# A two-layer diffusion backbone on one core: the order of the first loads and norm, and the place of the output stage against the second expert pass

## The reference, cut to what matters

```python
def _rms_norm(x, g):
    y = xf * lax.rsqrt(jnp.mean(xf * xf, axis=-1, keepdims=True) + EPS)
    return y * g
# every sub-layer: shift, scale, gate come from c and c_ctx
m = jax.nn.silu(cond) @ w + b            # (1024 x 6144) per layer, "modulation"
h = _rms_norm(x, g0) * (1 + scale) + shift
x = x + gate * _rms_norm(sublayer(h), g1)
# even layer: [short conv | latent attention], then dense SwiGLU
# odd layer: [differential attention | Fourier mixing], then top-2-of-8 experts
for e in range(N_EXPERTS):
    out = out + gates[..., e:e + 1] * _swiglu(h, w_gate[e], w_up[e], w_down[e])
```

## Time and profile before

| | us |
|---|---|
| median of 3 runs (lowest, highest) | 1734.29 (1732.22, 1735.79) |
| the profiled execution, its own time | 1732.53 |
| its span, first to last instruction | 1730.9 |
| PE busy | 1660.6, 96% of the span |
| DVE busy | 1061.8, 61% |
| ACT busy | 942.8, 54% |
| mean granted PE clock | 0.982 of full |

### The profile page before, as it was taken

One profiled execution on the slowest core, in us unless ns is written; L12 is line 12 of the kernel. 1 busy time (PEld: TensorE's weight loads), 2 busy tenths in 40 slices (PEclk: granted clock), 3 DMA queues, 4 the chain that ended last, 5 costly groups with the idle time before them and its releaser, 6 DMA issues.

```text
span 1730.9 us, 23094 instructions
## 1 busy us (share of the span) xinstructions
PE 1660.6 (96%) x8546; PEld 1323.4 (76%) x8546; DVE 1061.8 (61%) x1380; ACT 942.8 (54%) x1367; POOL 37.9 (2%) x60
## 2 busy tenths in 40 slices
PE   5898999999999999999988999999999999999997
PEld 2785458888888888678866788888888888888885
DVE  2341232253222233454474899999999989999997
ACT  3512333352222222363375677777777777777774
POOL 0000000030000000000000100000000000000010
PEclk9899899999999999999999999999999999999999
DMA  7523375169222222263204899999999999999991
GB/s 295 213 97 136 133 283 196 58 255 401 99 96 96 97 98 97 98 235 117 79 1 194 349 421 371 395 359 403 360 402 354 396 370 392 383 376 374 375 337 58
DMA packets 67708, 426.28 MB, mean 246 GB/s; under 512 B 8624, under 2 KB 12464, under 8 KB 19760
## 3 DMA queue, kind: packets, MB, share of 16 engines
q1 hardware_dynamic: 59856, 396.93, 59.8%
q0 software_dynamic: 7776, 28.32, 4.2%
HBM read 401.62 MB, written 23.59 MB: 246 GB/s over the span
## 4 chain that ended last, share of the span: by engine, by line
PE 91%; DVE 3%; ACT 3%; DMA 2%; issue 1%; SPq 0%; ACTq 0%; DVEq 0%
PE ps L1624 26%; PE ps L1626 26%; PE ps L1625 25%; PE ps L1642 3%; PE ps L1666 2%; PE ps L1781 2%; PE ps L1675 1%; DMA raw<-in_w 1%; PE ps L2063 1%; PE ps L1830 1%; DVE small L1184 1%; PE ps L1812 1%; DMA cst<-in_cst 1%; PE ps L1828 1%; DVE wl L982 1%
## 5 line engine op out<-in xcount | busy, mean ns | idle before, releaser
L1478 DVE TENSOR_TENSOR wl<-raw,wh 128x1024 fp32r<-128x1024 f32 x522 | 615.5, 1222 | 63.2 <-ACT wh L903 56.5
L903 ACT ACTIVATE wh<-raw 128x1024 fp32r<-128x1024 f32 x522 | 523.0, 1053 | 98.0 <-PE ps L1626 98.0
L1624 PE MATMUL ps<-wh,ah 128*128 128x512 f32 (+1 forms) x800 | 310.0, 387 | 1.8 <-ACT ah L886 1.2
L1624 PE MATMUL ps<-ah,wh 128*128 128x512 f32 (+1 forms) x848 | 301.1, 355 | 6.1 <-DVE al L1096 3.3
L1626 PE MATMUL ps<-wh,al 128*128 128x512 f32 (+1 forms) x800 | 302.3, 378 | 0.0
L1625 PE MATMUL ps<-wl,ah 128*128 128x512 f32 (+1 forms) x800 | 301.8, 377 | 0.0
L1626 PE MATMUL ps<-ah,wl 128*128 128x512 f32 (+1 forms) x848 | 293.6, 346 | 0.0
L1625 PE MATMUL ps<-al,wh 128*128 128x512 f32 (+1 forms) x848 | 293.6, 346 | 0.0
L982 DVE TENSOR_TENSOR wl<-raw,wh 128x1024 fp32r<-128x1024 f32 x120 | 141.5, 1222 | 126.3 <-ACT wh L480 126.3
L1624 PEld LDWEIGHTS ps<-ah,wh 128*128 128x128 f32 x848 | 161.4, 190 | 29.5 <-issue 4.1
L1625 PEld LDWEIGHTS ps<-al,wh 128*128 128x128 f32 x848 | 161.5, 190 | 20.4 <-issue 0.7
(11 more groups left out here) (251 smaller groups left out, 1584.1 us busy)
## 6 DMA issues: line engine op xcount, KB each, us to landing
raw<-in_w SPq DMA_DIRECT2D x372, 1024.0 KB, 6.4
sent<-raw POOLq DMA_DIRECT2D x16, 512.0 KB, 24.1
back<-raw POOLq DMA_DIRECT2D x16, 512.0 KB, 25.2
x<-sent POOLq DMA_DIRECT2D x7, 512.0 KB, 12.1
back<-x POOLq DMA_DIRECT2D x7, 512.0 KB
x<-in_x SPq DMA_DIRECT2D x1, 2048.0 KB, 11.4
raw<-in_ukv SPq DMA_DIRECT2D x1, 1024.0 KB, 7.4
out<-x SPq DMA_DIRECT2D x4, 256.0 KB, 2.4
```

Of the source, the lines that this page charges most:

```text
L903: act.activation(wh[:, J % SPLITS, piece_half(h)], slot(J % SLOTS)[:, piece_half(h)], ACT.Copy).then_inc(w_hi, 1)
L1478: ins = dve.tensor_tensor(wl[:, J % SPLITS, piece_half(h)], slot(J % SLOTS)[:, piece_half(h)], wh[:, J % SPLITS, piece_half(h)].bitcast(F3 ...
L1624: pe.matmul(out, lh, rh, start=start, stop=False)
```

## The change

In the start: `cst` is issued ahead of modulation piece 1; `x` goes behind modulation piece 2. PE takes the first norm's sums two at a time, ahead of modulation pieces 3, 4, 5 and 6, and a piece now goes ahead of the columns of the piece before it. ACT takes the lambda exponentials and row 2 ahead of the squares, rows 3 to 5 between the squares, and the high part of main piece 0 ahead of the root; DVE takes that piece's low part ahead of the root and the last three normalised chunks behind the scales. In the end: the output stage becomes a function `output(no)` that runs right behind `experts(0)`, ahead of the `If`; in the `If`'s body it runs again. The last down piece does column half 0 first and signals it (`y_half`), so ACT copies bank 3 earlier. The output's loops go by column half, then token half; the squares are over 512 columns, and the first half's sum enters the second half's Ln as its bias. The result goes to a slot of `raw` (`out_x`) instead of into `x`. `rows_final` is gone.

```diff
-                if p == 2:
+                if p == 1:
+                    sp.dma_start(cst[:, :, :], cst_d).then_inc(sem("cst_loaded"), 16)
+                if p == EARLY_SLOTS:
                     sp.dma_start(x[:, :, :], x_d).then_inc(x_loaded, 16)
-                    sp.dma_start(cst[:, :, :], cst_d).then_inc(sem("cst_loaded"), 16)
@@ ACT
-            act.wait_ge(x_loaded, 16)
-            squares(N_E1, lambda k: x[:, k, :])
             act.wait_ge(sem("lam_sums"), 1)
             act.activation(small[:, 2:4], ps[:, 5, 0:2], ACT.Exp).then_inc(sem("lam_exp"), 1)
+            rows(2)
+            act.wait_ge(x_loaded, 16)
+            for k in range(KD):
+                square(N_E1, k, x[:, k, :])
+                if k % 2 and k > 1:
+                    rows(2 + k // 2)
             act.wait_ge(consts_set, 1)
-            rows(2)
+            split(0)
             root(N_E1)
-            for n in range(3, MOD_FIRST - 2):
-                rows(n)
-            split(0)
...
+                    if banks == 2:
+                        act.wait_ge(w_used, PER_EXPERT * e + at.used + 2 + pieces)
+                    else:
+                        act.wait_ge(sem("y_half"), no + 1)
...
+            def output(no):
+                act.preload_act_table_set(LN_EXP)
+                for h in range(2):
+                    cols = slice(512 * h, 512 * h + 512)
+                    for t in range(2):
+                        act.wait_ge(sem("y_sum"), 4 * no + 2 * h + t + 1)
+                        act.activation(spare_row[:, t, cols], last_row[:, t, cols], ACT.Square, accum_out=half_ss[:, 2 * h + t:2 * h + t + 1]
+                                       ).then_inc(sem("y_ss"), 1)
+                        act.wait_ge(sem("y_ss"), 4 * no + 2 * h + t + 1)
+                        if h == 0:
+                            act.activation(half_eps[:, t:t + 1], half_ss[:, t:t + 1], ACT.Identity, bias=eps[:, 0:1], scale=1.0 / D
+                                           ).then_inc(sem("y_half_eps"), 1)
+                        else:
...
+                            act.activation(out_rinv[:, t:t + 1], half_ss[:, 2 + t:3 + t], ACT.Ln, bias=half_eps[:, t:t + 1], scale=1.0 / D
+                                           ).then_inc(sem("y_root"), 1)
...
+                            act.activation(out_rinv[:, t:t + 1], out_rinv[:, t:t + 1], ACT.Exp, scale=-0.5).then_inc(sem("y_root"), 1)
+                act.wait_ge(sem("y_root"), 4 * no + 4)
+                act.activation(last_row[:, 1, 0:512], last_row[:, 1, 0:512], ACT.Copy, scale=out_rinv[:, 1:2]).then_inc(sem("y_norm_act"), 1)
+
             experts(0)
+            output(0)
             with act.If(most > P):
+                act.preload_act_table(ACT.Silu)
                 experts(1)
...
+                output(1)
@@ DVE
+            split(0)
             inverse(N_E1)
             for k in range(KD):
+                if k == 5:
+                    dve.wait_ge(sem("mod_cols"), MOD_FIRST)
+                    take_modulation(0, 0, MOD_FIRST)
+                    scale_pre(0, 0, 8).then_inc(scales_ready, 1)
                 normed(N_E1, x[:, k, :], xn[:, k, :], k)
-            split(0)
-            dve.wait_ge(sem("mod_cols"), MOD_FIRST)
-            take_modulation(0, 0, MOD_FIRST)
-            scale_pre(0, 0, 8).then_inc(scales_ready, 1)
...
+            def output(no):
+                for h in range(2):
...
+                    for t in range(2):
+                        dve.wait_ge(sem("rows_summed"), 4 * no + t + 3)
+                        dve.wait_ge(sem("y_ps"), 4 * no + 2 * h + t + 1)
+                        dve.tensor_tensor(last_row[:, t, cols], last_row[:, t, cols], ps[:, OUT_BANKS[2 * t + h], :], ALU.add
+                                          ).then_inc(sem("y_sum"), 1)
+                for t, h in ((0, 0), (0, 1), (1, 1)):
+                    cols = slice(512 * h, 512 * h + 512)
+                    dve.wait_ge(sem("y_root"), 4 * no + 2 * t + 2)
+                    dve.tensor_scalar(last_row[:, t, cols], last_row[:, t, cols], out_rinv[:, t:t + 1], None, ALU.mult
+                                      ).then_inc(sem("y_norm_dve"), 1)
...
+                        dve.scalar_tensor_tensor(out=out_x[:, k, tk], in0=ps[:, TURN_BANKS[2 * t + k // 4], (k % 4) * P:(k % 4 + 1) * P],
+                                                 scalar=scl[:, 1, 3, k, 0:1], in1=x[:, k, tk], op0=ALU.mult, op1=ALU.add
+                                                 ).then_inc(sem("out_ready"), 1)
@@ PE
             mod_cols(0)
-            sum_squares(N_E1)
-            for n in range(2, MOD_FIRST):
+            def filler(n):
+                mod_piece(n)
                 mod_cols(n - 1)
-                mod_piece(n)
+            filler(2)
+            for n in range(3, MOD_FIRST):
+                if n < 7:
+                    sum_squares(N_E1, (2 * n - 6, 2 * n - 5))
+                filler(n)
...
+                    order = [(f, c) for c in range(2) for f in range(2)] if halves else [(f, c) for f in range(2) for c in range(2)]
+                    for f, c in order:
...
+                        if halves and (f, c) == (1, 0):
+                            mm.then_inc(sem("y_half"), 1)
...
+            def output(no):
...
+                for h in range(2):
+                    if h:
+                        pe.wait_ge(sem("y_rest"), no + 1)
+                    for t in range(2):
+                        pe.matmul(ps[:, OUT_BANKS[2 * t + h], :], back_sel_T[:, t * P:(t + 1) * P], y[:, 2 * h:2 * h + 2, :], start=True, stop=True
+                                  ).then_inc(sem("y_ps"), 1)
...
             experts(0)
+            output(0)
             with pe.If(most > P):
                 experts(1)
-            pe.wait_ge(sem("rows_final"), 1)
+                output(1)
```

More of the change, by code:

```diff
@@ L1528, in _ @@
             experts(0)
+            output(0)
             with dve.If(most > P):
+                dve.wait_ge(sem("y_ps"), 4)
                 dve.memset(back_sel_T, 0.0).then_inc(sem("back_sel_T"), 1)
+                dve.wait_ge(sem("y_root"), 4)
+                dve.memset(half_ss, 0.0).then_inc(sem("ss_cleared"), 1)
                 experts(1)
-                sum_rows(3)
-            dve.wait_ge(sem("back_sel_T"), 1)
-            dve.memset(small[:, 0:1], 0.0).then_inc(sem("rows_final"), 1)
@@ L1535, in _ @@
[L1535 to L1551, removed]
+                sum_rows(2)
@@ L2045, in gate_up, with down @@
                     mm.then_inc(w_used, 1)
-                def down(J, g, e):
+                def down(J, g, e, halves=False):
                     b = J % SPLITS
@@ L2050, in down @@
                     pe.wait_ge(sem("hT_lo"), 11 * e + (at.turned + g + 1))
[L2051 to L2054, removed]
-                                     wh[:, b, w0:w0 + 512], wl[:, b, w0:w0 + 512], g == 0 and f == 0, g == 10 and f == 1)
+                    order = [(f, c) for c in range(2) for f in range(2)] if halves else [(f, c) for f in range(2) for c in range(2)]
+                    for f, c in order:
+                        w0 = f * D + c * 512
+                        mm = mm3(ps[:, 3 + c, :], sh[:, g % 2, f * P:(f + 1) * P], sl[:, g % 2, f * P:(f + 1) * P],
+                                 wh[:, b, w0:w0 + 512], wl[:, b, w0:w0 + 512], g == 0 and f == 0, g == 10 and f == 1)
+                        if halves and (f, c) == (1, 0):
+                            mm.then_inc(sem("y_half"), 1)
                     mm.then_inc(w_used, 1)
@@ L2076, in body @@
                         else:
-                            down(J, g, e)
+                            down(J, g, e, order is LAST_ORDER and g == 10)
                         if q == GATHER and order is ORDER:
@@ L2086, in experts @@
                 if no:
-                    pe.wait_ge(sem("y_rest"), no)
+                    pe.wait_ge(sem("out_ready"), 16 * no)
                     gather(at.done)
@@ L2104, in experts @@
                 body(NE - 1, LAST_ORDER, LAST_TURN)
+            def output(no):
+                pe.wait_ge(sem("back_sel_T"), no + 1)
+                pe.wait_ge(sem("y_ready"), NE * (no + 1) + 1)
+                for h in range(2):
+                    if h:
+                        pe.wait_ge(sem("y_rest"), no + 1)
+                    for t in range(2):
+                        pe.matmul(ps[:, OUT_BANKS[2 * t + h], :], back_sel_T[:, t * P:(t + 1) * P], y[:, 2 * h:2 * h + 2, :], start=True, stop=True
+                                  ).then_inc(sem("y_ps"), 1)
+                for t in range(2):
+                    for k in range(KD):
+                        if (t, k) == (1, 0):
+                            pe.wait_ge(sem("y_norm_act"), no + 1)
+                        elif k % 4 == 0:
+                            pe.wait_ge(sem("y_norm_dve"), 3 * no + t + k // 4 + 1)
+                        mm = pe.transpose(ps[:, TURN_BANKS[2 * t + k // 4], (k % 4) * P:(k % 4 + 1) * P], last_row[:, t, k * P:(k + 1) * P], ident)
```

(20 more changed lines are left out.)

29 lines of the change are left out of this document (17 added, 12 removed).

## The result

| | before | after |
|---|---|---|
| median of the runs shown (lowest, highest), us | 1733.26 (1731.46, 1735.79) | 1721.01 (1718.90, 1721.32) |
| the profiled execution, its own time | 1732.53 | 1721.32 |
| its span | 1730.9 | 1719.8 |

The ratio is 0.9926, 95% interval 0.9914 to 0.9939: 0.74% faster. Forecast were 1721.5 and a range of 1717.5 to 1728.5.

What follows compares the result with a forecast made beforehand. TensorE holds 91% of the chain, so only the two ends can move: late loads at the start, a hole at the end. 1732.53 minus 7.7 and 5.1, less 1.76 to the median, gives 1721.5 us, range 1717.5 to 1728.5.

Steps and rivals of the forecast that it cites:

- The sum: Whole kernel: profiled 1732.53 minus 7.7 (start) and 5.1 (end) is 1719.7, plus 1.76 to the median: 1721.5 us.
- The start: Up to the first main matmul: last columns at 38.3 in place of 46.0, 7.7 us less, range 5.5 to 9.2.
- load 7: Start: load of modulation piece 7, issued when piece 5 is used (29.3), landing at 34.4 to 36.5.
- my lower bound of 5.05: Start: issue to use of a late load, 5.05 us into an empty queue, 7.2 with others in flight.
- The claim that the moved low part is free: Start, DVE: main piece 0's low part (2.4 us) moved ahead costs nothing as long as the last load is late.
- The forecast's weight on the clock: Start, TensorE: clock rises near 21.6; sums take 1.7 us before, 0.86 after; modulation pieces 1.94 and 1.07.
- The rival that breaking up the sums holds the clock down: Start: low clock throughout, columns at 47.05, 1.0 us later than before, total 1730.2; chance 0.08.
- The middle "runs on": Between the ends: TensorE runs on, a shift of the first main matmul goes through; the same 1662 us.
- The end: Behind the last expert matmul: residual instructions from 1718.75 to 1722.97 in place of 1728.07, 5.1 us less.
- The two are level, so up to 0.5 us could be lost: End: DVE's skip behind the output ends at 1725.5, the last store at 1725.8; up to 0.5 us lost.
- the hole: End: DVE's 2.57 us wait named "issue" and TensorE's 3.41 us idle ahead of the output, forecast to go.
- The second rival: End: the hole stays, only the output's finer order gains, 0.35 us; total 1726.2; chance 0.12.

Runs made afterwards that it cites:

- `head_only`: Only the start's hunks (loads, sums between pieces, low part ahead of the root) against the kernel before, end as before: 1723.95 us, 0.9948.
- `root_first`: Changed kernel with ACT's root put back ahead of main piece 0's high part, DVE's low part behind five normalised chunks: 1722.53 us, 0.9935 to the kernel before.
- `sums_at_once`: Changed kernel with all eight first-norm sums in one stretch ahead of modulation piece 3, rows 3 to 5 behind the squares: 1727.31 us, 0.9965 to the kernel before.
- `skip_first`: Changed kernel with the conditional body put back ahead of the output stage on ACT, DVE and TensorE: 1720.81 us, 0.9933 to the kernel before.
- `tail_only`: Only the end's hunks against the kernel before, start as before: 1728.20 us, 0.9971.

## Why the prediction was right, step by step

- *The sum.* 12.8 us were forecast from the two ends together and 12.7 measured. That this is so close is luck: the start gave 1.0 more and the end 1.1 less. What was right is each part's path; the sizes were off as follows. TensorE's 91% of the chain was no bar either: its own four products at the end took 1.7 us less, at the full level.
- *The start, 7.7 forecast, 8.7 measured* (6.8 in `head_only`). x at 17.0, the first pair from 17.75 and the steps of 3.4 us came within 0.2 us. Three terms were off. The clock rose at 23.4, 1.8 us later than assumed, and the first pair took 3.7 us (17.84 to 21.55), not 3.4, which put the issue of load 7 at 30.3, 1.0 late. Against that, load 7 took 4.8 us from issue to use (35.07), below my lower bound of 5.05, though load 6 was in flight beside it until 32.1; no run shows why. And piece 7 and the last columns ran at the full level, 2.2 us, where my bounds were 2.3 and 3.9. The claim that the moved low part is free was right, and `root_first` prices it at 2.0 us where it isn't hidden.
- *The forecast's weight on the clock* was sound in kind: a late load can cost twice, once as a wait and once at half speed behind it (2.43 us of wait in `head_only`, 6.09 in `sums_at_once`); behind the 0.93 of the changed kernel the level stayed full. The rival that breaking up the sums holds the clock down is out.
- *The middle "runs on"*: it does, within 3.4 us either way, for which the range had room but the text no word.
- *The end, 5.1 forecast, 4.0 measured.* "The residual instructions run from 1718.75", 7.1 us behind the copy: measured 6.4, as ACT's steps overlap: 0.75 us from a half square to its bias step and 0.21 from there to the next square, where I had 0.82 and 0.29. "The two are level, so up to 0.5 us could be lost" was the wrong step: 1.8 us are lost, and not by the skip that I watched. Leaving out DVE's skip brought 0.3, which the spread of 0.4 doesn't tell from nothing; TensorE's, which is off the path, costs 1.4 by its code fetches among the stores. I had read the skip only as a delay of the engine that skips.
- *What the hole was worth.* I put it at the head of the end's gain. `skip_first` shows that only 2.3 of the 5.8 us ahead of the residuals come from the skip's place. TensorE's matmuls follow each other across the skip there without a pause, which fits a skip made while queued matmuls still run; it stood still before because it waited for a cell written behind DVE's skip. The second rival, that the hole stays for any new code, is out: code in line had none.
- The Trainium skill ("Runtime: NRT & Kernel Launch", Instruction fetch mechanics) has a taken branch to code that isn't loaded pay for a fetch, and code in line fetched ahead: the traces agree, with 1.95 to 2.57 us on ACT and DVE in front and nothing in line; TensorE showed only a pause of 0.26 in its weight loads.

## What to carry to other kernels

When a few waits on a ring of load slots end a stage, put the work that needs something else (here the sums) between the uses that give slots back: the same work in one stretch cost 7.5 us here. A conditional body that is hardly ever taken has two prices, the skip on the engine and the code fetch on the DMA engines; place it where its engine is idle and no transfer is about to set the end, and check each engine by itself. A synchronising cell written by one engine behind such a skip makes all others pay for it.

## What the runs showed of the hardware

- With the skips behind the output, 1 MiB of closing stores ended 4.6 us behind the last residual instruction in place of 2.8, and a store behind each of TensorE's code fetches ended in a trickle; without TensorE's skip it was 3.2 and no trickle.
- TensorE skipped the body with a pause of 0.26 us in its weight loads and none in its matmuls, where ACT and DVE stood idle for 1.95 to 2.57.
- The granted clock reads 1.00 from 17 to 24 us in 13 of the 14 traces, while the first sum passes take twice as long as later ones; in `tail_only` it reads 0.50 until near 20 us, with the same durations. Ahead of the first recorded change only durations tell the level.
- One and the same order of work differs by up to 2.1 us at its start and 6.3 in its middle (1659.3 to 1665.6) from one execution to the next, with the times at which the clock rises and falls.
